# A compression in four column groups of the array, and weight rings moved by 64 bytes, in a two-layer encoder and decoder

## The reference

```
def nsa_compress(t, gidx, pe, w1, w2):          # t: one k or v stream, 64 wide; gidx: 15 windows of 32 tokens
    blocks = t[:, gidx] + pe
    flat = blocks.reshape(B, gidx.shape[0], NSA_CMP_LEN * HEAD_DIM)     # 15 x 2048
    return jax.nn.silu(flat @ w1) @ w2                                   # w1: 2048 x 256, w2: 256 x 64
...
k_cmp = nsa_compress(kc, gidx, cmp_pe[0], cmp_w1[0], cmp_w2[0])
v_cmp = nsa_compress(vc, gidx, cmp_pe[1], cmp_w1[1], cmp_w2[1])
```

## Time and profile before

| | |
|---|---|
| median of 3 runs | 1820.66 us |
| the profiled execution | 1819.93 us |
| its span | 1818.1 us |
| TensorE matmuls (PE) busy | 1796.5 us, 99% |
| VectorE (DVE), ScalarE (ACT) busy | 68%, 54% |
| DMA | 302.41 MB, mean 166 GB/s |

### The profile page before, as it was taken

One profiled execution on the slowest core, in us unless ns is written; L12 is line 12 of the kernel. 1 busy time (PEld: TensorE's weight loads), 2 busy tenths in 40 slices (PEclk: granted clock), 3 DMA queues, 4 the chain that ended last, 5 costly groups with the idle time before them and its releaser, 6 DMA issues.

```text
span 1818.1 us, 35757 instructions
## 1 busy us (share of the span) xinstructions
PE 1796.5 (99%) x15306; PEld 1712.9 (94%) x15306; DVE 1237.6 (68%) x1879; ACT 981.3 (54%) x1509; POOL 67.9 (4%) x32
## 2 busy tenths in 40 slices
PE   7999999999999999999999999999999999999999
PEld 7999998899999999999988999999989989989989
DVE  6775666765766567755767657665776678766777
ACT  6544567355644455444673555444655565556562
POOL 0000011500000000000115000000000000000000
PEclk9999999999999999999999999999999999999999
DMA  8555543243555655555433335565446435446332
GB/s 330 196 196 191 181 152 117 94 129 116 191 193 196 217 190 197 195 190 180 144 116 105 129 116 178 195 196 194 163 154 212 138 116 177 160 146 219 133 112 100
DMA packets 84462, 302.41 MB, mean 166 GB/s; under 512 B 9168, under 2 KB 11728, under 8 KB 84176
## 3 DMA queue, kind: packets, MB, share of 16 engines
q1 hardware_dynamic: 84304, 300.13, 49.6%
HBM read 299.04 MB, written 1.05 MB: 165 GB/s over the span
## 4 chain that ended last, share of the span: by engine, by line
PE 92%; DVE 6%; ACT 2%; issue 1%; DMA 0%; SPq 0%; DVEq 0%; ACTq 0%
PE bank L383 23%; PE bank L390 22%; PE bank L388 22%; PE bank L692 2%; DVE w_lo L1579 2%; PE bank L408 1%; PE bank L407 1%; PE bank L404 1%; PE bank L619 1%; PE bank L1018 1%; PE bank L451 1%; PE bank L1069 1%; PE bank L902 1%; PE bank L456 1%; PE bank L455 1%; PE bank L1039 1%
## 5 line engine op out<-in xcount | busy, mean ns | idle before, releaser
L1579 DVE TENSOR_TENSOR w_lo<-ring,w_hi 128x1024 fp32r<-128x1024 f32 x560 | 678.4, 1247 | 92.7 <-ACT w_hi L1135 91.5
L1135 ACT ACTIVATE w_hi<-ring 128x1024 fp32r<-128x1024 f32 x560 | 580.3, 1055 | 236.3 <-PE bank L383 196.7
L383 PE MATMUL bank<-xs,w_hi 128*128 128x256 f32 x2448 | 688.2, 281 | 0.0
L390 PE MATMUL bank<-xs,w_lo 128*128 128x256 f32 x2448 | 679.1, 277 | 0.0
L388 PE MATMUL bank<-xs,w_hi 128*128 128x256 f32 (+1 forms) x2454 | 679.1, 277 | 0.0
L383 PEld LDWEIGHTS bank<-xs,w_hi 128*128 128x128 f32 x2448 | 461.2, 188 | 4.1 <-issue 2.7
L388 PEld LDWEIGHTS bank<-xs,w_hi 128*128 128x128 f32 x2454 | 461.6, 188 | 3.2 <-issue 2.9
L390 PEld LDWEIGHTS bank<-xs,w_lo 128*128 128x128 f32 x2448 | 460.9, 188 | 0.0
L383 PE MATMUL bank<-a,w_hi 128*128 128x256 f32 x704 | 194.3, 276 | 0.0
L388 PE MATMUL bank<-a,w_hi 128*128 128x256 f32 x704 | 194.3, 276 | 0.0
L390 PE MATMUL bank<-a,w_lo 128*128 128x256 f32 x704 | 194.3, 276 | 0.0
(11 more groups left out here) (399 smaller groups left out, 3079.1 us busy)
## 6 DMA issues: line engine op xcount, KB each, us to landing
ring<-in_w SPq DMA_DIRECT2D x560, 512.0 KB, 3.3
arena<-in_mem SPq DMA_DIRECT2D x2, 1024.0 KB, 12.5
const<-in_const SPq DMA_DIRECT2D x1, 1395.0 KB, 15.6
h<-in_x SPq DMA_DIRECT2D x1, 768.0 KB, 7.7
out<-h SPq DMA_DIRECT2D x3, 256.0 KB, 2.5
dec_par<-in_dec SPq DMA_DIRECT2D x1, 615.0 KB, 19.4
h<-in_x SPq DMA_DIRECT2D x1, 256.0 KB, 4.7
out<-h SPq DMA_DIRECT2D x2, 128.0 KB, 2.0
```

The source lines that it names most:

```text
L383: last = nc.tensor.matmul(o, wh, hi(x, k0 + k), start=k == 0, stop=False, skip_group_check=True)
L390: last = nc.tensor.matmul(o, wl, hi(x, k0 + k), start=False, stop=k == nk - 1, skip_group_check=True)
L1135: nc.scalar.activation(w_hi[:, s * UNIT:(s + 1) * UNIT], ring[:, u % RU, :], AF.Copy).then_inc(sems("w_hi"), 1)
L1579: nc.vector.tensor_tensor(w_lo[:, r * UNIT:(r + 1) * UNIT], ring[:, r, :], w_hi[:, s * UNIT:(s + 1) * UNIT].bitcast(F32), ALU.subtract).th ...
```

## The change

Compression: `flat` gets 32 columns per offset and stays plain f32. Its matmuls take the weights as they lie in the ring, unrounded, in one plain f32 matmul for each offset; offset l goes to the 32 array columns that begin at (l mod 4) x 32, and so to partitions 32 x (l mod 4) and on of bank 5. Thus four partial sums arise, which the matmul with `two32` (now 32 columns wide, a one where row mod 32 equals the column) adds up while it turns them; SiLU comes behind that. The units of the compression (`WHOLE`, 8 a layer) are left out by ScalarE's and VectorE's rounding, and the slots of `w_hi` and the counts of its semaphores go by the number of the unit among the others (`NTH`, `SPLIT`). Where ScalarE was led through the eight units one by one, it now has three calls of `highs`.

Addresses: both rings begin 192 bytes behind a multiple of 256, xs and the other activations stay 64 behind (`parts` rounds to 256 bytes now).

```diff
-                cmpn=2 * NCMP, cmpm=2 * NCMP, two8=8, two18=18, two32=8, cos=T, sin=T, final=KD)
+                cmpn=2 * NCMP, cmpm=2 * NCMP, two8=8, two18=18, two32=32, cos=T, sin=T, final=KD)
+WHOLE = frozenset(DEC0 + l * DEC_UNITS + U_CMP + n for l in range(LAYERS) for n in range(8))
+SPLIT = [u for u in range(UNITS_ALL) if u not in WHOLE]
+NTH = {u: n for n, u in enumerate(SPLIT)}
...
+        sb("ring_pad", 16)
         ring_at = here()
...
+        if (64 - here()) % 256:
+            sb("xs_pad", (64 - here()) % 256 // 4)
...
-        assert ring_at % 128 == 0 and hi_at % 128 == 0 and xs_at % 128 == 64 and arena_at % 128 == 64
+        assert ring_at % 256 == 192 and hi_at % 256 == 192 and xs_at % 256 == 64 and arena_at % 256 == 64
...
-            n0 = at[0] = -(-at[0] // 32) * 32
+            n0 = at[0] = -(-at[0] // 64) * 64
...
+            def whole(self, wide):
+                u, pos = divmod(self.n, UB)
+                if pos == 0:
+                    self.w.e.wait_ge(sems(f"landed{u % RU}"), 16 * (u // RU + 1))
+                self.n += wide
+                return ring[:, u % RU, pos * P:(pos + wide) * P], pos == 0
...
-                pe.e.wait_ge(*pe.need('flat_lo', 1))
+                pe.e.wait_ge(*pe.need('flat', 4))
                 for l in range(32):
-                    wh, wl, first = w.two(2)
-                    fh, fl = (f[:, l * 2 * NCMP:(l + 1) * 2 * NCMP] for f in (flat_hi, flat_lo))
-                    o = bank[5][0:2 * NCMP, 0:T]
-                    last = nc.tensor.matmul(o, fh, wh, start=l == 0, stop=False, skip_group_check=True)
+                    g = l % 4 * 32
+                    ws, first = w.whole(2)
+                    last = nc.tensor.matmul(bank[5][g:g + 32, 0:T], flat[:, l, :], ws, start=l < 4, stop=l >= 28,
+                        skip_group_check=True)
                     if first:
                         last.then_inc(sems("unit_begun"), 1)
-                    nc.tensor.matmul(o, fl, wh, start=False, stop=False, skip_group_check=True)
-                    last = nc.tensor.matmul(o, fh, wl, start=False, stop=l == 31, skip_group_check=True)
...
-                    last = nc.tensor.transpose(bank[6][:, ht * 2 * NCMP:(ht + 1) * 2 * NCMP],
-                        hid_t[0:2 * NCMP, ht * P:(ht + 1) * P], ident[0:2 * NCMP, 0:2 * NCMP])
+                    last = nc.tensor.matmul(bank[6][:, ht * 2 * NCMP:(ht + 1) * 2 * NCMP],
+                        hid_g[:, ht * P:(ht + 1) * P], C('two32')[:, 0:2 * NCMP], start=ht == 0, stop=True,
+                        skip_group_check=True)
...
-                    if True:
-                        s = u % HU
+                    if u not in WHOLE:
+                        n = NTH[u]
+                        s = n % HU
...
-                a.e.wait_ge(*a.need('flat', 4))
-                nc.scalar.activation(tiles(flat_hi[:, :], 32), flat, AF.Copy).then_inc(*a.tell('flat_hi'))
...
-                for n in range(1, 9):
-                    s.ahead(u0 + U_CMP + n)
+                s.highs(u0 + U_GL + 2)
                 a.e.wait_ge(*a.need('hid_full', 1))
-                nc.scalar.activation(hid_t[0:2 * NCMP, :], bank[5][0:2 * NCMP, 0:T], AF.Silu).then_inc(*a.tell('hid_s'))
+                nc.scalar.activation(hid_g, bank[5][:, 0:T], AF.Copy).then_inc(*a.tell('hid_s'))
+                s.highs(u0 + U_GL + 3)
                 a.e.wait_ge(*a.need('hid_turned', 1))
-                nc.scalar.activation(hid, tiles(bank[6][:, 0:4 * NCMP], 2), AF.Copy).then_inc(*a.tell('hid_e'))
+                nc.scalar.activation(hid, tiles(bank[6][:, 0:4 * NCMP], 2), AF.Silu).then_inc(*a.tell('hid_e'))
...
-                for n in range(1, 9):
-                    w.ahead(u0 + U_CMP + n)
+                w.lows(u0 + U_GL + 3)
```

More of the change, by code:

```diff
@@ L93 @@
               pt="v_sb", f_sq="v_sb", q_sq="ab", q_ln="zl", q_rstd="b_e", masks="l_sb", v="y0", fv="a_sb",
-              gf="o_out", gate_e="o_sq", ft="os_out", flat_hi="os_rstd", z_out="ys", hid_s="l_sq",
+              gf="o_out", gate_e="o_sq", ft="os_out", z_out="ys", hid_s="l_sq",
               hid_e="gz_e", kc_sq="l_ln", vc="l_rstd", forget_hi="dte", kcs_ln="eg", kcs_rstd="yy",
@@ L98 @@
               f_ss="sp_sb", raw="sp_sb", qn="g_out", q_sin="y", qr="gcol", flat="dt", xf="mixed", lf="k_out",
-              flat_lo="qkn", z_r="rr", gl_e="kb", fcol="kq", kcn="kend", kc="lt", pc_d="qkd", pcn="xt_up",
+              z_r="rr", gl_e="kb", fcol="kq", kcn="kend", kc="lt", pc_d="qkd", pcn="xt_up",
               nm="x_up", ob="r1", up_out="mix_lo")
 FFN_UNITS = 3 * KF
+WHOLE = frozenset(DEC0 + l * DEC_UNITS + U_CMP + n for l in range(LAYERS) for n in range(8))
+SPLIT = [u for u in range(UNITS_ALL) if u not in WHOLE]
+NTH = {u: n for n, u in enumerate(SPLIT)}
 class Counts:
@@ L224, in build_program @@
         ident, ones, bones, le = C("ident"), C("ones"), C("bones"), C("le")
-        if (64 - here()) % 128:
-            sb("arena_pad", (64 - here()) % 128 // 4)
+        if (64 - here()) % 256:
+            sb("arena_pad", (64 - here()) % 256 // 4)
         arena_at = here()
-        assert ring_at % 128 == 0 and hi_at % 128 == 0 and xs_at % 128 == 64 and arena_at % 128 == 64
+        assert ring_at % 256 == 192 and hi_at % 256 == 192 and xs_at % 256 == 64 and arena_at % 256 == 64
         room = (nc.sbuf_bytes_remaining // 4 // 8) * 8 - 64
@@ L325, in build_program @@
         forget_r = rounded("forget", T, arena_at + 4 * at[0])
-        flat_hi = rounded("flat_hi", 64 * NCMP, arena_at + 4 * pairs_at)
         kvc = take(T)
@@ L329, in build_program @@
         zb = take(8, T)
-        flat_lo = rounded("flat_lo", 64 * NCMP, arena_at + 4 * at[0])
-        flat, hid, hid_t = take(32, 2 * NCMP), take(2, 2 * NCMP), take(T)
+        flat, hid, hid_g = take(32, 32), take(2, 2 * NCMP), take(T)
         kc, kcr, kcs, krt, vc = take(NCMP), take(NCMP), take(NCMP), take(NCMP), take(64)
@@ L358, in low_ready @@
             def low_ready(self, u):
-                self.w.e.wait_ge(sems("w_lo"), u + 1)
+                self.w.e.wait_ge(sems("w_lo"), NTH[u] + 1)
+            def whole(self, wide):
[4 more added lines that the diff above has]
+                return ring[:, u % RU, pos * P:(pos + wide) * P], pos == 0
             def two(self, wide=1):
@@ L368, in two @@
                 self.n += wide
-                c, d = (u % HU * UB + pos) * P, (u % RU * UB + pos) * P
+                c, d = (NTH[u] % HU * UB + pos) * P, (u % RU * UB + pos) * P
                 return w_hi[:, c:c + wide * P], w_lo[:, d:d + wide * P], pos == 0
@@ L1575, in lows @@
                 for u in range(self.u, min(upto, UNITS_ALL)):
-                    if True:
-                        s, r = u % HU, u % RU
-                        self.w.e.wait_ge(sems("w_hi"), u + 1)
+                    if u not in WHOLE:
+                        s, r = NTH[u] % HU, u % RU
+                        self.w.e.wait_ge(sems("w_hi"), NTH[u] + 1)
                         nc.vector.tensor_tensor(w_lo[:, r * UNIT:(r + 1) * UNIT], ring[:, r, :],
@@ L1958, in hybrid_dve @@
                             in1=r1, op0=ALU.mult, op1=ALU.mult).then_inc(*d.tell())
-                d.e.wait_ge(*d.need('flat_hi', 1))
-                nc.vector.tensor_tensor(tiles(flat_lo[:, :], 32), flat, tiles(flat_hi[:, :], 32).bitcast(F32),
-                    ALU.subtract).then_inc(*d.tell('flat_lo'))
                 for j in range(4):
@@ L2205, in constants @@
     put("causal", np.where(np.concatenate([low, low], 1), 0.0, -BIG))
-    put("two32", row % 32 == col[:, :8])
+    put("two32", row % 32 == col[:, :32])
     end = np.arange(NCMP) * 16 + 31
```

4 lines of the change are left out of this document (2 added, 2 removed).

## The result

The changed kernel takes 1860.24 us (median of 4), the kernel before 1820.29 beside it: 1.022 times as long, 95% interval 1.0205 to 1.0240. Forecast were 1801.5, so the sign was wrong: 40 us slower. The profiled execution has a span of 1858.4 us.

A forecast was written before the change was run, and what follows sets the result against it. TensorE's busy time was taken as the bound. From 1819.93 us, 14.1 went for the compression half in two layers and 5 for the addresses, giving 1800.8, or 1801.5 to the median; range 1774 to 1824.

The forecast's parts named there:

- The bound: Whole kernel: TensorE is busy 99% of the span, so only TensorE time taken away counts, not ScalarE or VectorE savings.
- The compression: Decoder layers: 32 plain f32 matmuls in four overlapping column groups take 3.65 us a layer instead of 11.12, plus 0.2 wait.
- rival 4: Compression: column groups overlap by two only, 6.9 us a layer (chance 0.08), or not at all, 13.7 (chance 0.03).
- The two-group rows: Attention values: two column groups' f32 matmuls took 0.80 us against 1.29 in sequence; four were taken to overlap likewise.
- The turn: Hidden layer: two transposes become two f32 matmuls that add up the four groups, costing 0.2 us more a layer.
- The kc chain: ScalarE's small kc operations, behind four roundings, end near 13.1 us, covered by 0.3; at risk 0 to 2 us a layer.
- The addresses: All matmuls: moving the weight rings from 128 to 192 bytes behind multiples of 256 was put at -5 us.
- Rival 3: FFN stretches: the new offset makes the slow step of 0.1179 the rule, 1825 with half, 1845 with all; chance 0.17.
- Rival 1: Addresses: the offset does nothing, since the moment a stretch begins sets its step; 1806.5 us, chance 0.22.

The follow-up runs named there:

- groups_only: The changed kernel with the rings put back to 128 bytes behind multiples of 256, the old distance of 64 to the activations; 1804.16 us, ratio 0.9907 to 0.9957.
- no_split: groups_only without the 128-column pieces at the second matmul of some groups; 1827.06 us, ratio 1.0034 to 1.0087 against the kernel before.
- split_more: groups_only with the 128-column pieces also in the q and k projections; 1806.08 us, ratio 0.9908 to 0.9953 against the kernel before.
- dist_48: The changed kernel with rings 112 bytes behind multiples of 256 and activations 64, a distance of 48; 1863.6 us, ratio 1.0169 to 1.0294.
- thin_64: groups_only with each matmul behind a sum's first, in tile-by-tile projections, cut to 32 of 256 moving columns; 2824.4 us, the clock mostly at 0.50.
- thin_0: The same thinned moving stream as thin_64, but with rings and activations both 64 bytes behind, distance 0; 2827.9 us, the clock mostly at 0.50.

## Why the prediction was wrong

**The bound**: right. PE's time alone counted: what PE was spared accounts for all that groups_only gained (below), and nothing is left for the 16 roundings fewer on each of two engines.

**The compression**: right in mechanism and size. Forecast were 3.65 us and a wait of 0.2, together 3.85; it is 3.81 with a wait of 0.15 in groups_only, and 3.82 in the second layer of the changed kernel:

```profile
1391.93 3.66 PE L950 MATMUL bank<-ring,arena 128*32 128x256 f32 x64
1395.74 0.36 PE L403 MATMUL bank<-xs,w_hi 128*128 128x256 f32 x1 [0.15 <-DVE w_lo L1597]
```

The 4.21 in the first layer of the changed kernel lie outside the 3.6 to 3.9 of the forecast, by the landing of unit 40. Forecast was a landing 0.6 us behind the compression's start; in groups_only it came 0.7 behind it, here 1.7, since the transfer took 4.4 us from its issue and not 3.2. ScalarE's rounding of unit 40 waited for it:

```profile
1441.08 1.06 ACT L1152 ACTIVATE w_hi<-ring 128x1024 fp32r<-128x1024 f32 x1 [0.29 <-DMA ring<-in_w]
```

The 64 records start in fours, 6 to 8 ns apart within a four, and behind the first a four begins every 0.216 us. A round of four matmuls of two records each takes 0.432, as long as one matmul alone: the groups overlap by four, and rival 4 (6.9 us or more) is refuted. The two-group rows showed the way. The estimate by the Trainium skill, page "TensorE: Matmul & The Clock Gate", section "Part 3: Packing small matmuls", was 4.3 us for the eight rounds; the trace has 3.66 with the drain of the last.

**The turn**: forecast 0.2 us more a layer. From its first matmul to the next one of the stream it takes 0.37 against 0.23. But before the change there was a gap of 0.21 ahead of the two transposes (1406.23 to 1406.44) where the stream's step is 0.12, and it is gone (1446.34 to 1446.46), so the turn costs 0.04 more in all. Before:

```profile
1406.23 0.28 PE L390 MATMUL bank<-xs,w_lo 128*128 128x256 f32 x1
```

and in the changed kernel:

```profile
1446.34 0.28 PE L407 MATMUL bank<-xs,w_lo 128*128 128x256 f32 x1
1446.46 0.53 PE L970 MATMUL bank<-const,arena 128*128 128x30 f32 x4
1446.83 0.37 PE L400 MATMUL bank<-xs,w_hi 128*128 128x256 f32 x1
```

**The kc chain**: right. ScalarE did the four roundings and then the kc operations, done 13.4 us behind the compression's start (forecast 13.1), and no wait of PE on it shows. (Between the sum and the kc operations it does five roundings, units 42 to 46, and not four as was said under the order lists; the prediction rightly counts four, as unit 42 comes ahead of the turned copy.)

```profile
1448.56 4.03 ACT L1152 ACTIVATE w_hi<-ring 128x1024 fp32r<-128x1024 f32 x4
1452.49 0.16 ACT L1482 ACTIVATE arena<-bank 128x15 f32<-128x15 f32 x1
1452.55 0.18 ACT L1483 ACTIVATE arena<-bank 128x15 f32<-128x15 f32 x1
```

The whole of this half was forecast at -14.1 us and measured at -14.4 (the ratio's interval allows -8 to -17). The traces give the same per layer: 11.12 - 3.81, less 0.09 for the way in, which the change of shape makes longer, less 0.04 for the turn, is 7.18, for two layers 14.4. So this is no luck of two errors.

**The addresses**: here the prediction failed, at the words "I take -5 us". The term is +54. The step of reasoning that failed is the choice of a value "nearest" to the fast row: 0.1133 in the FFN was read as what a stream does when nothing is in its way, and 0.1178 as the disturbance that a new distance might cure. In truth 0.1133 was the fast of two states, held by a distance that had to be exact to less than 16 bytes and, at that distance, by how a stretch began. Nine of the ten distances tried are worse and none is better, so a move away from it was far more likely to lose than to gain. Rival 3 (chance 0.17, at most 1845) was the right mechanism, mis-sized: it took 0.1179 as the slowest step there is, and counted 8300 matmuls, leaving out those on other activations (ob, mg and more) and under other lines. With 5.3 ns more (0.1187) on those 8300 it is 44 us, and the traces have some 11,550 such steps, not 9462. The range of 1774 to 1824 left most of this rival out.

Seen from here, two things in the trace of before pointed to it. In the decoders stretches of 46 matmuls stay at one of two steps, at one and the same distance: so 0.1133 is one of two states that the streams keep up, and can be lost as well as won. And the FFN's window stands at the faster of the two, which leaves that stretch nothing to gain and much to lose.

Rival 1 (the offset is worth nothing) is refuted: the offset is worth 54 us. Its other half, that the moment at which a stretch begins chooses between two steps, holds at the distance of 64 in so far as the beginning chooses (no_split, split_more). TensorE's moving stream and its weight loads slow each other here, by 1.7 to 11.7 ns on top of the 111.7 of a load. The Trainium skill, page "SBUF — State Buffer", section "SBUF: two separate sides", says that TensorE never waits on anyone; for its own two streams this does not hold here.

**Open**: why 64 is the good distance and what the ten steps are made of. That the two streams meet in the memory is a guess: no run looks there, and no model was found that gives 0.1200 at 0, 0.1133 at 64 and 0.1187 at 80. Whether the nudge works by the time that it shifts or by the extra load was not tried. The second states, at 64 and at others (0.1187 and 0.1200 in the changed kernel's own FFN), say that the step is a function of distance and history, not of distance alone.

## What to carry to other kernels

Where TensorE is fed back to back with float32r weights and activations, measure the distance between the starts of two matmuls of one form in several stretches before touching anything that moves a buffer: a pad of 64 bytes cost 3% here, nearly four times what the change of the same patch that works gained. When a layout changes, pin the old distance first, and time the layout by itself, in several executions, since one stretch may fall into another step from one to the next. Small plain-f32 matmuls with few stationary columns are worth putting into four column groups: four ran in the time of one.

## What the runs showed of the hardware

- Step of a float32r matmul of 256 columns with its load of 128: 0.1133 (groups_only) to 0.1233 us (dist_48) at full clock, by the distance of the two operands modulo 256 bytes and by how the stretch began; the load alone 0.112 (thin_64, thin_0).
- Four column groups of 32: 64 records of plain f32, 256 columns, in 3.66 us; one group at a time would be 13.7, an estimate from 0.43 for one.
- With 32 moving columns for each load of 128 the granted clock fell to 0.50 though PE was busy all the time, and the step rose from 0.112 to 0.213 us (thin_64). So the load takes longer at the lower clock, too.
